# Closing stages of a two-block decoder kernel: evictions scaled in place, sums of squares and update terms held in PSUM, chunks split over their own columns only, the square root's table loaded ahead

## What is computed

```
def _rmsnorm(x, g):
    y = xf * lax.rsqrt(jnp.mean(xf * xf, axis=-1, keepdims=True) + EPS)
    return (y * g.astype(jnp.float32)).astype(x.dtype)
...
x = x + 0.5 * rms_norm(swiglu(rms_norm(x, nw[0]), ffn_w_gate[l, 0], ffn_w_up[l, 0], ffn_w_down[l, 0]), nw[1])
x = x + rms_norm(m, nw[3])
```

## Time and profile before

| | us |
|---|---|
| median of three runs | 3993.34 |
| range of the three | 3988.49 to 3994.52 |
| the profiled execution, its time | 3997.27 |
| its span | 3995.5 |
| TensorE busy (share of the span) | 3743.4 (94%) |
| VectorE busy | 1852.2 (46%) |
| GpSimd busy | 1363.5 (34%) |
| ScalarE busy | 1254.8 (31%) |

### The profile page before, as it was taken

One profiled execution on the slowest core, in us unless ns is written; L12 is line 12 of the kernel. 1 busy time (PEld: TensorE's weight loads), 2 busy tenths in 40 slices (PEclk: granted clock), 3 DMA queues, 4 the chain that ended last, 5 costly groups with the idle time before them and its releaser, 6 DMA issues.

```text
span 3995.5 us, 54705 instructions
## 1 busy us (share of the span) xinstructions
PE 3743.4 (94%) x20771; PEld 3180.1 (80%) x20771; DVE 1852.2 (46%) x2349; ACT 1254.8 (31%) x1996; POOL 1363.5 (34%) x547
## 2 busy tenths in 40 slices
PE   8888899999998899999998999998999888889998
PEld 8776699999984788888887788887888766568887
DVE  2562235445455455562327652226232689644225
ACT  3532222222224222232223442224222333633222
POOL 3221134444330244434443124443444400043443
PEclk9988899999998799999999999999999999999999
DMA  3110022222220122222222112222222222022222
GB/s 144 64 64 32 22 72 82 90 90 90 80 69 1 43 90 95 95 82 94 93 95 90 38 64 90 95 95 79 95 95 95 80 71 71 7 90 69 95 95 84
DMA packets 86569, 307.96 MB, mean 77 GB/s; under 512 B 9584, under 2 KB 11888, under 8 KB 86256
## 3 DMA queue, kind: packets, MB, share of 16 engines
q1 hardware_dynamic: 85968, 304.28, 22.1%
q10 hardware_dynamic: 416, 1.05, 0.1%
HBM read 303.19 MB, written 2.10 MB: 76 GB/s over the span
## 4 chain that ended last, share of the span: by engine, by line
PE 78%; issue 9%; DVE 8%; ACT 2%; DVEq 2%; POOL 0%; ACTq 0%; DMA 0%; SPq 0%; POOLq 0%
PE psum L364 64%; PE psum L636 4%; PE psum L674 1%; DVE resid L885 1%; PE psum L1390 1%; DVE arena L1161 1%; PE psum L1377 1%; DVE arena L1266 1%; DVE square_sum L860 1%; PE psum L654 1%; PE psum L933 1%; PE psum L1621 1%; PE psum L1879 1%; DVEq L884 1%; PE psum L946 1%
## 5 line engine op out<-in xcount | busy, mean ns | idle before, releaser
L328 POOL TENSOR_TENSOR w_lo<-w_raw,w_hi 128x1024 fp32r<-128x1024 f32 x484 | 1212.4, 2506 | 2344.7 <-ACT w_hi L320 2344.7
L320 ACT ACTIVATE w_hi<-w_raw 128x1024 fp32r<-128x1024 f32 x508 | 537.9, 1059 | 1901.8 <-PE psum L364 1889.7
L364 PE MATMUL psum<-x_hi,w_hi 128*128 128x512 f32 (+1 forms) x2744 | 908.7, 360 | 43.3 <-DVE w_lo L2474 31.7
L364 PE MATMUL psum<-x_lo,w_hi 128*128 128x512 f32 (+1 forms) x2744 | 905.5, 358 | 0.0
L364 PE MATMUL psum<-x_hi,w_lo 128*128 128x512 f32 (+1 forms) x2744 | 901.2, 357 | 0.0
L364 PE MATMUL psum<-y_hi,w_hi 128*128 128x264 f32 (+1 forms) x2288 | 641.3, 331 | 40.0 <-DVE arena L1298 17.6
L364 PE MATMUL psum<-y_lo,w_hi 128*128 128x264 f32 (+1 forms) x2288 | 642.4, 331 | 0.0
L364 PE MATMUL psum<-y_hi,w_lo 128*128 128x264 f32 (+1 forms) x2288 | 639.3, 330 | 0.0
L364 PEld LDWEIGHTS psum<-x_hi,w_hi 128*128 128x128 f32 x2744 | 488.9, 189 | 133.1 <-DVE w_lo L2474 38.0
L364 PEld LDWEIGHTS psum<-x_lo,w_hi 128*128 128x128 f32 x2744 | 486.5, 189 | 78.8 <-issue 1.4
L364 PEld LDWEIGHTS psum<-x_hi,w_lo 128*128 128x128 f32 x2744 | 487.3, 189 | 76.9
(11 more groups left out here) (449 smaller groups left out, 4379.9 us busy)
## 6 DMA issues: line engine op xcount, KB each, us to landing
w_raw<-in_weights SPq DMA_DIRECT2D x567, 512.0 KB, 3.2
resid<-in_xT SPq DMA_DIRECT2D x8, 264.0 KB, 7.9
out_dram<-resid SPq DMA_DIRECT2D x16, 128.0 KB, 1.7
arena<-in_lru_w SPq DMA_DIRECT2D x1, 1024.0 KB, 10.1
rope_sb<-in_rope SPq DMA_DIRECT2D x1, 528.0 KB, 11.7
mats<-in_mats SPq DMA_DIRECT2D x1, 512.0 KB, 10.2
rope_sb<-in_rope ACTq DMA_DIRECT2D x1, 512.0 KB, 4.1
y_space<-in_pool_inv ACTq DMA_DIRECT2D x1, 512.0 KB, 4.7
```

Of the source, the lines that this page charges most:

```text
L320: nc.scalar.activation(weight_parts(n, i, c)[0], RAW[:, (n + c) % 4, :], ACT.Copy).then_inc(high_ready, 1)
L328: nc.gpsimd.tensor_tensor(wl, RAW[:, (n + c) % 4, :], wh, ALU.subtract).then_inc(low_ready, 1)
L364: last = mm(o[:, a, :], wt[:, k * P:k * P + P], x[:, k, a * (w // banks):(a + 1) * (w // banks)], start=(k == 0 and p == 0), stop=(k == kt ...
```

## The change

It has four parts, all in or for the closing stages. (1) `finish` multiplies in place in PSUM and adds from there. (2) The sums of squares are kept in PSUM bank 7 (`G[:, 7, :]`) and only the last add of each half (m = 7 and 11) writes `ACC` in SBUF, from which TensorE sums. The update's term is written to the unused half of the PSUM bank that holds the spread scale; since there is now one place for it per half, a `drain()` stands before it. (3) `SPLIT_COLS` gives chunks n+2 to n+7 of each closing kt x 128 columns, 768 for kt=6; ScalarE and GpSimd split only these. (4) A square root of one column stands at the head of `close_act`'s pieces.

```
+            for i in range(2, 8):
+                SPLIT_COLS[n + i] = kt * P
...
-            nc.scalar.activation(weight_parts(n, i, c)[0], RAW[:, (n + c) % 4, :], ACT.Copy).then_inc(high_ready, 1)
+            w = SPLIT_COLS.get(at, DT * P)
+            nc.scalar.activation(weight_parts(n, i, c)[0][:, 0:w], RAW[:, (n + c) % 4, 0:w], ACT.Copy).then_inc(high_ready, 1)
...
-                nc.gpsimd.tensor_tensor(wl, RAW[:, (n + c) % 4, :], wh, ALU.subtract).then_inc(low_ready, 1)
+                w = SPLIT_COLS.get(n + 4 * i + c, DT * P) if isinstance(i, int) else DT * P
+                nc.gpsimd.tensor_tensor(wl[:, 0:w], RAW[:, (n + c) % 4, 0:w], wh[:, 0:w], ALU.subtract).then_inc(low_ready, 1)
...
-                dst = ACC if f == 0 else SQ[f % 2]
+                dst = G[:, 7, :] if f == 0 else SQ[f % 2]
                 nc.scalar.activation(dst[:, c], src[f][:, c], ACT.Square).then_inc(squared, 1)
...
+            nc.scalar.activation(SCOL[:, 7:8], ones[:, 0:1], ACT.Sqrt)
             for f in range(4):
...
-                tt(ACC[:, c], ACC[:, c], SQ[f % 2][:, c], ALU.add).then_inc(added, 1)
+                out = ACC[:, c] if m in (7, 11) else G[:, 7, c]
+                tt(out, G[:, 7, c], SQ[f % 2][:, c], ALU.add).then_inc(added, 1)
...
-                t = SCR[:, 2, half(m % 2)]
+                t = G[:, 6 + h, HALF:T2]
+                dve.drain()
                 stt(t, y[:, f, c], g[f], ps, ALU.mult, ALU.mult)
                 dve.drain()
                 tt(r[f][:, c], r[f][:, c], t, ALU.add).then_inc(updated, 1)
...
-                t = SCR[:, 4 + f % 2, c]
-                tt(t, ps, RS[:, c], ALU.mult)
-                dve.drain()
-                return tt(YF[:, f, c], YF[:, f, c], t, ALU.add)
+                tt(ps, ps, RS[:, c], ALU.mult)
+                dve.drain()
+                return tt(YF[:, f, c], YF[:, f, c], ps, ALU.add)
```

More of the change, by code:

```diff
@@ L256, in build @@
                    "f2p": ("ffn2_down2", 6), "oddp": ("o_out_y", 8), "f3p": ("ffn3_down2", 6)}
-        RESIDENT, FREE_AT = {}, {}
-        for name, (stage, _) in CLOSING.items():
+        RESIDENT, FREE_AT, SPLIT_COLS = {}, {}, {}
+        for name, (stage, kt) in CLOSING.items():
             n = CHUNKS[stage]
+            for i in range(2, 8):
+                SPLIT_COLS[n + i] = kt * P
             slots5 = [(RES[:, 2 * i, :], RES[:, 2 * i + 1, :]) for i in range(5)]
@@ L1077, in finish_part @@
             def finish_part(ps, f, c):
-                t = SCR[:, 4 + f % 2, c]
-                tt(t, ps, RS[:, c], ALU.mult)
+                tt(ps, ps, RS[:, c], ALU.mult)
                 dve.drain()
-                return tt(h[:, f, c], h[:, f, c], t, ALU.add)
+                return tt(h[:, f, c], h[:, f, c], ps, ALU.add)
             if l:
```

## The result

The changed kernel took 3971.48 us in the median (3967.85 to 3977.44, five runs) beside 3994.52 for the kernel before on the same chip: a ratio of 0.995, 95% interval 0.9937 to 0.9963. A second comparison later, six runs beside nine of the kernel before, gave 3975.45 beside 3987.49, ratio 0.9965 (0.9953 to 0.9978). So the gain is 12 to 23 us by the medians, 0.35 to 0.5%; the forecast was 19 us, and a time of 3974.

The account below looks back on a forecast made before the run. TensorE was taken as most of the chain, waiting in closings for VectorE instructions blocked by GpSimd subtracts. Terms -21.9, +1.0 and +1.8 sum to -19.1 us, from 3993.34 to 3974; range 3964 to 3985.

Parts of the forecast that it names:

- The main term: f0p, f1p, f2p, first half pass to next stage's first matmul: PSUM operands cut each to 20.2 us, -21.9 us in all.
- The estimate of 0.5 us: Added to each of the three windows: 0.16 for the new drain, 0.3 for VectorE's lost slack between last evictions.
- The update: Stage behind a closing: the block moves from the add to the low part; only 0.3 us at most saved.
- The +0.2 for each of five closings: Early waits for low parts in first_halves: drains cost 0.45, less 0.3 saved; taken as +0.2 each, +1.0 us together.
- The drain: New drain in update(): 0.16 us each where VectorE is the bound; fourteen in f3p, +2.2 less 0.44, so +1.8 us.
- The 0.44 for the two waits: f3p: waits of 0.28 and 0.16 us, the second for the reciprocal behind the table load, would go.
- Splits and table: 768-column splits and earlier table load in the closings: 0 for the splits; the load's gain in other terms, its price 0.
- (a): VectorE reading and writing one PSUM bank pays 0.27 us more per instruction; net +11 us, 4004; 4%.
- (b): Half clock stays in the three closings, 3.4 us each return, 3984; same price for GpSimd's late start; 14%.
- (c): More comes back: no half clock anywhere, L892 escapes one of two blocks, five closings win 1.5 us more; 3966; 10%.
- (d): Skill page's rules: PSUM sources cost 62 cycles more, 3977, 6%; the drain is free, 3971, 4%.
- (e): VectorE is late for another reason than the operands; stalls stay, only the drains count, +4 us, 3997; 2%.

Follow-up runs that it names:

- e1: Kernel before with only the evictions and the sums of squares in PSUM; 3970.98 us in one run beside 3987.72.
- e8: Kernel before with only the evictions in PSUM, sums of squares left in SBUF; 3986.44 us in a single run beside 3990.3.
- e9: Kernel before with only the sums of squares in PSUM, evictions' adds left in SBUF; 3983.60 us in a single run beside 3987.49.
- e7: Changed kernel with the update's term back in scratch, without the drain, and two splits moved; 3960.57 us beside 3990.3, ratio 0.9922.
- e4: Kernel before with only the table load ahead; closings in sum 367.5 us, against 369.7 before.
- e5: Changed kernel with only the update's term back in its two scratch halves, without the drain; closings in sum 346.1 us, against 349.7 changed.
- e3: Kernel before with only the update's term in PSUM and its drain; closings in sum 370.3 us, against 369.7 before.
- e6: Changed kernel with only the two splits moved, drain kept; closings in sum 343.7 us, against 349.7 changed.
- e2: Kernel before with only the splits over 768 columns; closings in sum 363.2 us, against 369.7 before.

## Why the prediction was right, point by point

*The main term.* Three windows of 20.2 us were forecast, 20.0 came: 22.5 us won for 21.9. That GpSimd's subtract blocks a VectorE instruction with two SBUF inputs is now shown from both sides, and not only read off two lines: e1, e8 and e9 move one operand to PSUM and the blocks go, e7 leaves the operands in SBUF and moves the subtract, and they go too. The estimate of 0.5 us behind f3p's 18.4 was sound: the wait for the first low part went from 1.28 to 1.80.

*The update.* "This will not be won" held: the block moved from the add to the low part, and the stretches behind stayed at 30.2 in f0p. The +0.2 for each of five closings, 1.0 in all, was mis-sized: from first half pass to the last one behind, evenp and oddp moved by -0.1 and +0.1, and the stretches behind f0p, f1p and f2p by 0, +0.2 and 0. Together +0.2. Behind f0p the two early waits grew from 1.27 and 1.53 us to 1.46 and 1.73, near the 0.45 forecast, and the wait behind the blocks fell from 0.80 to 0.38, where 0.3 was forecast as saved: the two cancel.

*The drain.* 0.16 was forecast where VectorE is the bound, 0.18 measured: the multiply with its result in PSUM takes 489 ns, not 475. f3p lost 2.4 us, not 1.8, and the term that was too small is the drains'. The 0.44 for the two waits was won: without the drain, e4 and e5 end f3p 0.6 us earlier than before, 35.7 for 36.3. The drain and the PSUM term cost 2.8 (e3) to 3.0 us (e5; e7 beside e6), not 2.2: from update(2) to update(15) VectorE takes 14.1 us instead of 11.7, and 0.4 to 0.6 more is lost ahead of update(2), which the forecast, counting from there, left out. In the changed kernel update(2) starts 21.4 us behind the first half pass, as before the change; in e5 it starts after 20.8. The sum over all terms is -19.9 against -19.1.

*Splits and table.* Both were put at 0 beside the PSUM operands. e5 with both is 1.8 us shorter than e1 with neither, 0.2 to 0.5 us in each of the three windows and 0.5 in f3p. Part of that the forecast had inside its other terms, as the wait behind the table load; which of the two edits brings how much of it in the windows, no run tells.

*The rivals.* (a) One bank for reading and writing costs 8 to 14 ns, not 270. (b) The half clock did not stay in the three windows (1.00). It did appear behind f0p, where it cost nothing (30.2 with it and without), since TensorE waits there anyway, and behind f1p, where it can have cost at most the 0.2 above. (c) did not come by itself: 12 low parts are blocked; e7 had to move the splits for it. (d) An instruction with a PSUM input and an SBUF result takes 422, against 426 before with two SBUF inputs. The Trainium skill ("VectorE: DVE Perf Modes", the section on the TRN2 errata) had 62 cycles more for it; no run shows that. By its section "The DRAIN you can't avoid", as the prediction read it, the new drain would be free; the step contradicts that, 1.08 us for 0.90. The prediction left out that this section also says that a next instruction that is not held starts earlier, and the rows agree with that part: 0.35 us after the start of an add of 0.43. (e) is excluded by e1.

## What to carry to other kernels

When an instruction's mean is far above its minimum, look at the maximum by source line and at what runs beside it; the blocked form is told from the free one by where its operands lie. Freeing the instruction that is blocked only moves the block if its neighbour has the same form, so count the operands of what comes next, or move the other engine's work to where nobody of that form runs. Read a small gain in stretches that repeat: here the closings of one kernel repeat to 0.1 us in sum while whole runs differ by 10. Where engines stall the stretches repeat less well, some of them only to 1 us.

## What the runs showed that I had not expected

The time outside the closings follows the half-clock stretches. In thirteen traces it goes from 3614.7 us, with 225.3 us outside the closings granted at 1.2 GHz (e2), to 3627.6 with 259.4 (e8), nearly on a line: a straight line through all thirteen rises by 0.34 us per microsecond at half clock. The kernel before's first profile (259.4, 3625.8) lies at its slow end and the changed one's (232.1, 3616.9) near the other; what places these stretches in unchanged code, no run tells.

Writing PSUM was nearly free on VectorE: a result in PSUM instead of SBUF adds 10 ns to a tensor-tensor of 256 columns (422 to 433) and 14 to the multiply. On ScalarE it saves: the first square of a closing, 512 columns, took 602 ns into PSUM and 632 into SBUF.
